# Last layer's output projection as seven block products instead of eight, with the weight sums on GpSimd and VectorE

## The reference, cut to what matters

```python
for l in range(DEPTH):                       # DEPTH = 2
    xn = rms_norm(h, norm_g[l])
    proj = xn @ w_in[l]
    ...                                      # three head groups: ya, yb, yc; gates ga, gb, gc
    mixed = concatenate([ya * silu(ga), yb * silu(gb), yc * silu(gc)])
    h = h + mixed @ w_out[l]                 # (528 x 2048) @ (2048 x 2048)
return h[:, REAL_START:]                     # the 512 real positions only
```

## Time and profile before

| | us |
|---|---|
| median of 3 runs (lowest, highest) | 1549.18 (1548.6, 1549.85) |
| span of the profiled execution | 1547.2 |
| TensorE busy | 1537.9 (99%) |
| VectorE busy | 949.6 (61%) |
| ScalarE (ACT) busy | 646.1 (42%) |
| GpSimd (POOL) busy | 197.0 (13%) |
| DMA traffic over the span | 97 GB/s |

### The profile page before, as it was taken

One profiled execution on the slowest core, in us unless ns is written; L12 is line 12 of the kernel. 1 busy time (PEld: TensorE's weight loads), 2 busy tenths in 40 slices (PEclk: granted clock), 3 DMA queues, 4 the chain that ended last, 5 costly groups with the idle time before them and its releaser, 6 DMA issues.

```text
span 1547.2 us, 26370 instructions
## 1 busy us (share of the span) xinstructions
PE 1537.9 (99%) x10458; PEld 1423.5 (92%) x10458; DVE 949.6 (61%) x1829; ACT 646.1 (42%) x1291; POOL 197.0 (13%) x348
## 2 busy tenths in 40 slices
PE   8999999999999999999999999999999999999999
PEld 7999999999999999999998889888999888888888
DVE  5787788677778444343336676876777774442322
ACT  5776566612333332322236665666132343221211
POOL 0112654400000000000000016544000000000000
PEclk9999999999999999999999999999999999999999
DMA  7222111223221322443342231121223123234442
GB/s 279 102 83 82 56 55 58 73 74 99 82 84 55 105 86 97 139 151 124 130 146 86 82 109 56 55 78 60 86 80 110 55 82 109 82 133 141 142 146 69
DMA packets 39739, 151.79 MB, mean 98 GB/s; under 512 B 5424, under 2 KB 14400, under 8 KB 24896
## 3 DMA queue, kind: packets, MB, share of 16 engines
...
## 4 chain that ended last, share of the span: by engine, by line
PE 96%; DVE 1%; issue 1%; POOL 1%; ACT 1%; DMA 0%; ACTq 0%; DVEq 0%; POOLq 0%
PE ps_gemm L1144 82%; PE ps_mix L1031 3%; PE ps_mix L950 2%; PE ps_mix L996 2%; PE ps_gemm L911 2%; PE ps_mix L964 2%; PE ps_gemm L1105 1%; PE ps_gemm L898 1%; PE ps_mix L898 1%; PE ps_mix L992 1%; PE ps_mix L1074 1%; PE ps_mix L1089 1%; PE ps_mix L1091 0%; DMA w_stage<-in_w_in 0%; PE ps_mix L977 0%
## 5 line engine op out<-in xcount | busy, mean ns | idle before, releaser
L1144 PE MATMUL ps_gemm<-x_hi,w_hi 128*128 128x264 f32 (+3 forms) x2176 | 542.2, 314 | 0.2 <-issue 0.2
L1144 PE MATMUL ps_gemm<-x_hi,w_lo 128*128 128x264 f32 (+3 forms) x2176 | 528.3, 308 | 0.0
L1144 PE MATMUL ps_gemm<-x_lo,w_hi 128*128 128x264 f32 (+3 forms) x2176 | 527.6, 307 | 0.0
L1144 PEld LDWEIGHTS ps_gemm<-x_hi,w_hi 128*128 128x128 f32 x2176 | 353.8, 189 | 19.8 <-issue 0.6
L1144 PEld LDWEIGHTS ps_gemm<-x_hi,w_lo 128*128 128x128 f32 x2176 | 352.1, 188 | 19.3
L1144 PEld LDWEIGHTS ps_gemm<-x_lo,w_hi 128*128 128x128 f32 x2176 | 351.5, 188 | 16.8
L647 ACT ACTIVATE w_hi<-w_stage 128x512 fp32r<-128x512 f32 x464 | 267.1, 618 | 172.0 <-DVE z L1309 122.8
L1216 DVE TENSOR_TENSOR w_lo<-w_stage,w_hi 128x512 fp32r<-128x512 f32 x392 | 259.5, 690 | 82.2 <-ACT w_hi L647 76.3
L1144 PE MATMUL ps_gemm<-mixed_hi,w_lo 128*128 128x264 f32 (+1 forms) x752 | 199.0, 320 | 0.0
L1144 PE MATMUL ps_gemm<-mixed_lo,w_hi 128*128 128x264 f32 (+1 forms) x752 | 198.7, 320 | 0.0
L1144 PE MATMUL ps_gemm<-mixed_hi,w_hi 128*128 128x264 f32 (+1 forms) x752 | 197.6, 318 | 0.0
...
## 6 DMA issues: line engine op xcount, KB each, us to landing
w_stage<-in_w_in SPq DMA_DIRECT2D x82, 1024.0 KB, 4.9
w_stage<-in_w_out SPq DMA_DIRECT2D x32, 1024.0 KB, 5.4
...
a_rden<-rden SPq DMA_DIRECT2D x32, 128.0 KB, 5.0
...
```

The source lines that it names most:

```text
L1144: ins = pe.matmul(g[:, bank, 0:size], ws, xs[:, k, c:c + size], start=tick == 0 and i == 0, stop=tick == TICKS - 1 and i == 2)
```

## The change

In the last layer (`FAST`) the output projection is no longer a run of chunks. The weight is cut into 8 pairs p of row blocks (output channels 256p to 256p + 255), each pair into four quarters of 128 output channels by 1024 contraction rows (A11, A12, A21, A22; 512 KB each). The data is cut the same way, contraction halves (`K_FIRST`, `K_SECOND`) by time halves of 256 positions (B11, B12, B21, B22). Each pair is then made from seven block products of 8 x 3 matmuls of 256 columns, in place of eight (a Winograd variant of Strassen's form):

- sums of the data, made once: T1 = B12 - B11 (VectorE, in `gate_product`, in the place of B12), T2 = B22 - T1 and T4 = B21 - T2 (GpSimd, `t_raws`), T3 = T2 - B11 (GpSimd, `t3_raw`);
- sums of the weights, for each pair: S1 = A21 + A22, S3 = A11 - A21, S4 = A12 - S2 (GpSimd, `sum_1`, `sum_3`, `sum_4`), S2 = S1 - A11 (VectorE, `sum_2`);
- the products, in this order: A11 B11, S1 T1, S2 T2, S4 B22, S3 T3, A12 B21, A22 T4. Bank x gathers A11 B11, S2 T2, S3 T3 and A22 T4 one on the other, bank z S1 T1 and S4 B22; VectorE takes the bank out after each of them (`product_out`, 7 for a pair) and adds it to the residual or to what stands in z.

Each of the seven weights goes through a high part on ACT (`out_high`) and a low part on VectorE (`out_low`), now in one piece of 1024 columns each; so do T2, T3, T4 (`t_high`, `t_low`). The raw quarters and sums lie in a ring of 12 places, the high parts in one of 4. The eager order of all this around the last gate chunk (N = 99) and in pair 0 is written out by hand. The diff, cut to its core:

```diff
--- before.py
+++ after.py
-NTOT = DEPTH * NC
...
+FAST = DEPTH - 1
+NTOT = NC * FAST + N_IN
+HALF_K = KC // 2
+K_FIRST, K_SECOND = GATES[:HALF_K], GATES[HALF_K:]
+PAIRS = KC // 2
+HALF_T = SEQ // 2
+PRODUCTS = ("a11", "s1", "s2", "s4", "s3", "a12", "a22")
+NPROD = len(PRODUCTS)
+RING, HI_RING = 12, 4
+RING_AT = {"a11": 0, "s1": 1, "a21": 2, "s3": 2, "a22": 3, "s2": 4, "a12": 5, "s4": 6}
...
+        def bank_of(p, which):
+            b = (3 * p + "xzy".index(which)) % 4
+            return G[:, b // 2, b % 2, 0:HALF_T]
...
+            sp.wait_ge(s_gemm, NTOT - 2)
+            load_quarter(0, "a21")
+            load_quarter(0, "a22")
+            sp.wait_ge(s_gemm, NTOT - 1)
+            load_quarter(0, "a11")
+            sp.wait_ge(s_xfree, 1)
+            load_quarter(0, "a12")
+            load_quarter(1, "a11")
...
+            sp.wait_ge(s_hy, 4 * DEPTH)
+            load_res(0, 0)
+            load_res(0, 1)
+            sp.wait_ge(s_gemm, NTOT)
+            load_quarter(1, "a21")
+            sp.wait_ge(s_t3r, 2)
+            sp.wait_ge(s_tlo["t2"], 2)
+            load_quarter(1, "a22")
+            for p in range(PAIRS):
+                if p + 1 < PAIRS:
+                    sp.wait_ge(s_made, made(p, "a11"))
+                    load_quarter(p + 1, "a12")
+                sp.wait_ge(s_out, made(p, "s2"))
+                if p + 1 < PAIRS:
+                    load_res(p + 1, 0)
+                if p + 2 < PAIRS:
+                    load_quarter(p + 2, "a21")
+                sp.wait_ge(s_out, made(p, "s4"))
+                store_quarter(p, 0, 1)
+                if p + 2 < PAIRS:
+                    sp.wait_ge(s_made, made(p, "s3"))
+                    load_quarter(p + 2, "a11")
+                sp.wait_ge(s_out, made(p, "s3"))
+                store_quarter(p, 1, 1)
+                if p + 2 < PAIRS:
+                    sp.wait_ge(s_made, made(p, "a12"))
+                    load_quarter(p + 2, "a22")
+                sp.wait_ge(s_out, made(p, "a12"))
+                store_quarter(p, 0, 0)
+                sp.wait_ge(s_out, made(p, "a22"))
+                store_quarter(p, 1, 0)
+                if p + 1 < PAIRS:
+                    load_res(p + 1, 1)
+            for i in range(2):
+                for j in range(2):
+                    sp.wait_ge(s_q[i][j], 16 * PAIRS)
...
+            def t_raws(N):
+                zi, j = N % 2, K_SECOND.index(gate_of(N % NC))
+                m = K_FIRST[j]
+                if j == 0:
+                    pool.wait_ge(s_hy, 4 * DEPTH)
+                    pool.wait_ge(s_rdm, 8 * DEPTH)
+                    pool.wait_ge(s_rdo, 16 * DEPTH)
+                pool.wait_ge(s_prod, KC * FAST + HALF_K + j + 1)
+                pool.wait_ge(s_mlo, KC * FAST + j + 1)
+                z1, z2 = zq(zi, 0), zq(zi, 1)
+                link(pool.tensor_tensor(t2r[:, j], z2, mh[:, m, t_half(1)].bitcast(F32), ALU.subtract))
+                link(pool.tensor_tensor(t2r[:, j], t2r[:, j], ml[:, m, t_half(1)].bitcast(F32), ALU.subtract))
+                pool.tensor_tensor(t4r[j // 4][:, j % 4], z1, t2r[:, j], ALU.subtract).then_inc(s_traw, 1)
+            def t3_raw(half):
+                js, ms = slice(4 * half, 4 * half + 4), slice(K_FIRST[4 * half], K_FIRST[4 * half] + 4)
+                if half == 0:
+                    pool.wait_ge(s_gemm, NTOT)
+                link(pool.tensor_tensor(t3r[:, js], t2r[:, js], mh[:, ms, t_half(0)].bitcast(F32), ALU.subtract))
+                link(pool.tensor_tensor(t3r[:, js], t3r[:, js], ml[:, ms, t_half(0)].bitcast(F32), ALU.subtract))
+                pool.sem_inc(s_t3r, 1)
+            def sum_1(p):
+                pool.wait_ge(s_ld["a21"][p % 2], 16 * (p // 2 + 1))
+                pool.wait_ge(s_ld["a22"][p % 2], 16 * (p // 2 + 1))
+                if p >= 2:
+                    pool.wait_ge(s_made, made(p - 2, "a22"))
+                else:
+                    pool.wait_ge(s_gemm, NTOT - 1 + p)
+                pool.tensor_tensor(raw_of(p, "s1")[:], raw_of(p, "a21")[:], raw_of(p, "a22")[:], ALU.add)\
+                    .then_inc(s_sum["s1"], 1)
...
+            def sum_3(p):
+                pool.wait_ge(s_ld["a11"][p % 2], 16 * (p // 2 + 1))
+                pool.wait_ge(s_sum["s1"], p + 1)
+                pool.tensor_tensor(raw_of(p, "s3")[:], raw_of(p, "a11")[:], raw_of(p, "a21")[:], ALU.subtract)\
+                    .then_inc(s_sum["s3"], 1)
+            def sum_4(p):
+                pool.wait_ge(s_ld["a12"][p % 2], 16 * (p // 2 + 1))
+                pool.wait_ge(s_sum["s2"], p + 1)
+                if p:
+                    pool.wait_ge(s_made, made(p - 1, "s1"))
+                else:
+                    pool.wait_ge(s_xfree, 1)
+                pool.tensor_tensor(raw_of(p, "s4")[:], raw_of(p, "a12")[:], raw_of(p, "s2")[:], ALU.subtract)\
+                    .then_inc(s_sum["s4"], 1)
...
+                    if layer == FAST and tick == T_RAW_TICK and n and gate_of(n - 1) in K_SECOND:
+                        t_raws(N - 1)
+                if N == NTOT - 1:
+                    sum_1(0)
+                    sum_3(0)
+                    sum_4(0)
+            t3_raw(0)
+            t_raws(NTOT - 1)
+            t3_raw(1)
+            for p in range(1, PAIRS):
+                sum_1(p)
+                sum_3(p)
+                sum_4(p)
...
+            def out_high(p, name):
+                no = made(p, name) - 1
+                if name in s_sum:
+                    act.wait_ge(s_sum[name], p + 1)
+                else:
+                    act.wait_ge(s_ld[name][p % 2], 16 * (p // 2 + 1))
+                if no >= HI_RING:
+                    act.wait_ge(s_made, no - HI_RING + 1)
+                else:
+                    act.wait_ge(s_gemm, NTOT - 1 + no // 2)
+                act.activation(high[no % HI_RING], raw_of(p, name)[:], ACT.Copy).then_inc(s_ohi, 1)
...
+            out_high(0, "s1")
+            out_high(0, "a11")
+            act.wait_ge(s_xfree, 2)
+            act.wait_ge(s_traw, HALF_K - 1)
+            t_high("t2", 0, HALF_K - 1)
+            out_high(0, "s2")
+            N = NTOT - 1
+            zz = zs(N % 2)[:, N_META:T]
+            act.wait_ge(s_z, N + 1)
+            act.activation(ta_[:, N_META:T], zz, ACT.Tanh, scale=0.5).then_inc(s_th, 1)
+            out_high(0, "s4")
+            act.wait_ge(s_prod, KC * DEPTH)
+            act.activation(mh[:, GATES[-1], N_META:T], zz, ACT.Copy).then_inc(s_mhi, 1)
+            act.wait_ge(s_traw, HALF_K)
+            t_high("t2", HALF_K - 1, HALF_K)
+            act.wait_ge(s_t3r, 1)
+            t_high("t3", 0, 4)
+            out_high(0, "s3")
+            t_high("t4", 0, 4)
+            t_high("t4", 4, 8)
+            act.wait_ge(s_t3r, 2)
+            t_high("t3", 4, 8)
+            out_high(0, "a12")
+            out_high(0, "a22")
+            for p in range(1, PAIRS):
+                for name in PRODUCTS:
+                    out_high(p, name)
...
+            def product(p, name):
+                which, cols, moving = {"a11": ("x", 0, "first"), "s1": ("z", 1, "first"), "s2": ("x", 0, "t2"),
+                                       "s4": ("z", 1, "second"), "s3": ("x", 0, "t3"), "a12": ("y", 0, "second"),
+                                       "a22": ("x", 0, "t4")}[name]
+                no = made(p, name) - 1
+                pe.wait_ge(s_olo, no + 1)
+                if name == "a11" and p >= 2:
+                    pe.wait_ge(s_out, made(p - 2, "a12"))
+                if name == "s1" and p:
+                    pe.wait_ge(s_out, made(p - 1, "a22"))
+                if name in ("s2", "s4", "s3"):
+                    pe.wait_ge(s_out, no - 1)
+                if name == "a12":
+                    if p:
+                        pe.wait_ge(s_out, made(p - 1, "s4"))
+                    else:
+                        pe.wait_ge(s_z, NTOT)
+                if name == "a22":
+                    pe.wait_ge(s_out, made(p, "s3"))
+                start = name in ("a11", "s1", "a12")
+                o = bank_of(p, which)
+                hi, lo = high[no % HI_RING], low[ring_at(p, name)]
+                for j in range(HALF_K):
+                    if moving in th_:
+                        if p == 0 and j in (0, 4, 7):
+                            pe.wait_ge(s_tlo[moving], {0: 1, 4: 1 if moving == "t2" else 2, 7: 2}[j])
+                        xs, ys = th_[moving][:, j], tl_[moving][:, j]
+                    else:
+                        m = (K_FIRST if moving == "first" else K_SECOND)[j]
+                        if p == 0 and name == "s4" and j == HALF_K - 1:
+                            pe.wait_ge(s_mlo, KC * DEPTH)
+                        xs, ys = mh[:, m, t_half(cols)], ml[:, m, t_half(cols)]
+                    for i, (ws, vs_) in enumerate(((hi[:, j], xs), (hi[:, j], ys), (low[ring_at(p, name)][:, j], xs))):
+                        ins = pe.matmul(o, ws, vs_, start=start and j == 0 and i == 0,
```

(92 more changed lines are left out.)

111 lines of the change are left out of this document (69 added, 42 removed).

## The result

The kernel after takes 1555.79 us (median of 4 runs, 1554.67 to 1556.41), the kernel before on the same chip 1548.89 (4 runs, 1547.36 to 1549.85): a ratio of 1.0043, 95% interval 1.0031 to 1.0055. The forecast was 1554.5. The profiled execution has a span of 1553.9 us (1547.2 before).

The account below looks back on a forecast made before the run. TensorE, busy 99% of the span, was taken as the bound. The terms -19.1 + 22.2 + 1.5 + 0.8 = +5.4 us took the median from 1549.18 to about 1554.5, range 1538 to 1563.

Parts of the forecast that it names:

- the turns: VectorE operations with two SBUF inputs and GpSimd sums exclude each other, each for a whole operation; said to decide the forecast.
- the walk: Diff's order timed operation by operation through the projection's start: TensorE begins 8.2 us after 1366.1, pair 1 at 1408.2.
- the signs named in advance: Pair 0 stretched to 34 us, out_low and t_low up to 3.5 us beside sums of up to 3.6.
- TensorE's own work: Projection matmuls: 178.2 us removed, 159.1 added, net -19.1 us if every product finds its operands ready.
- The beginning: Projection's start, pair 0: sums and low parts made in turns while TensorE needs only 19.9 us; 22.2 us lost.
- Pair 1 and the clock: Pair 1's start: 1.5 us where sum_1(2) cuts in before S1's low part, 0.8 for TensorE's lowered clock.
- The edits that cost nothing: Gate slots and tail: T1's subtracts (8 x 0.42 us) and t_raws fall in idle time; tail as before.
- The smaller tile: Projection matmuls of 256 columns: half the columns cost 51% of the time, taking back 3.5 of 22.3 us.
- The first: Rival: engines don't exclude each other at these places; VectorE alone paces the beginning, -12.5 us, 1536.7; chance 0.15.
- The second: Rival: GpSimd's float32 sums run at the fast rate, 1.9 us for 1024 columns; 1547, halfway 1550.5; chance 0.20.
- The third: Rival: turns bind in every pair, 20.5 to 21.2 us instead of 19.9; 1558 to 1563; chance 0.15.
- The fourth: Rival: the whole 19.1 us saving of the projection arrives; 1530; chance 0.02.

Follow-up runs that it names:

- Experiment 1: Kernel after, but out_low, t_low and sum_2 read their second input from PSUM (other data) instead of SBUF: 1540.91 us, 0.9944 of before.
- 4: Kernel after with T3's four GpSimd subtracts cut to 4 columns, T3's parts made from T4's tile: 1549.39 us, one run.
- 2: Kernel after with S1, S3, S4 and T3 computed on VectorE, its order changed too: 1546.24 us, 0.9980 of before.
- experiment 3: Kernel after without the eight T1 subtracts in gate_product, B12 standing in for T1: 1555.22 us, one run.
- 5: Kernel with S1, S3, S4 and T3 on VectorE, pair 0 now done as eight plain block products: 1539.46 us, 0.9935 of before.
- experiment 6: Kernel with the plain first pair, pair 1's A11 low part now made first in its own buffer, S3 later: 1538.46 us, 0.9928 of before.

## Why the prediction was right

**The step that decides, the turns.** It was taken from pieces of 512 columns for pieces of 1024 and 1792. Every time of the walk came 0.9 to 1.4 us after its forecast, a nearly constant shift from the first entry on: S1 done at 1364.3 (forecast 1363.1), S4 at 1370.2 (1369.0), the first half of T3 at 1374.3 (1373.1), TensorE's start at 1375.4 (1374.3), pair 1 at 1409.3 (1408.2). From S1 to pair 1 the walk had 45.1 us and the trace has 45.0. Experiment 1 shows the mechanism, 4 that the length of that exclusive work sets the end, and in 2, with the sums on one engine, the low parts are back at 1.23 on average. The turns don't fill the whole stretch: GpSimd sat idle 3.95 us, until 1394.61, for the load of pair 1's weights and 5.45 us before S4 of pair 1, while VectorE worked on alone. The walk has both (`sum_1(1)` ends at 1396.0 there, at 1397.0 in the trace). The widest rows were longer than the signs named in advance, 4.03 for the 3.5 of `t_low` and 4.12 for the 3.6 of a sum, where each waited for a full operation of the other engine. The rule of the Trainium skill (SBUF — State Buffer, Who interferes with whom: an operation with at most one SBUF input doesn't contend, one with two contends with GpSimd's reads, and the port pair is an exclusive lock) held at the widths seen here, 512 to 1792 columns: for 1024 columns 1.22 us in experiment 1 against a mean of 1.75 in the kernel after.

**The terms of the sum.** In the projection the forecast was -19.1 + 22.2 + 1.5 + 0.8 = +5.4; the trace has 183.73 - 178.16 = +5.6.
- TensorE's own work: -19.1 forecast, -18.3 measured (eight steady pairs of 19.98). The steady pitch is 0.1189, not the 0.1184 of `last_block`, 0.08 us a pair, 0.7 in all; a product is 2.84 to 2.88.
- The beginning: 22.2 forecast. Measured 8.3 before the first product and 33.86 - 19.98 = 13.9 of stretch in pair 0, together 22.2.
- Pair 1 and the clock: 1.5 + 0.8 forecast; pair 1 lost 21.69 - 19.98 = 1.7. The clock did fall to its lower level, before the first product and near the end of the pair, and A11's product took 5.28 us and A22's 4.42. But both lie in pair 0, where VectorE was later still; the 0.8 put ahead for pair 1's start did not come here (it did in experiments 2 and 5, where A11's product in pair 1 took 4.24 and 5.28). The two errors, +0.8 in TensorE's own work and -0.6 here, nearly cancel: that the sum is off by only 0.2 is partly luck.
- "The edits that cost nothing": this step failed. T1's subtracts were costed at 0 because VectorE sits idle before each take-out of a gate chunk. That is true around the last gates, but the earlier ones lie beside the attention, where TensorE waits for VectorE; experiment 3 shows 1.4 to 1.5 us of the 3.4. In the profiled execution 0.5 of it is hidden by a start that was 0.5 earlier than in before's. So the change of the span is 6.7: 1.5 - 0.5 ahead of the projection, 5.6 in it, and 0.1 in the tail; and the median came 1.3 above the forecast.
- Two smaller slips change nothing in the sum. The smaller tile takes back 22.3 - 19.1 = 3.2 us, not 3.5. And GpSimd's 2.15 ns a column stands in no row of the kernel before; the kernel after bears it out, with 0.74 us for 256 columns and 2.40 for 1024.

**The rivals.** The first (no exclusion, 1536.7) is nearly what experiment 1 built: 1540.9. Its first product came 4.3 us after the gate, not 3.6, and the clock fell there too (0.81 from 1366 to 1375, A11's product 4.50 us), which the rival's sum left out. The second, GpSimd at its fast rate, is out: 2.40 by itself, for 2.38 forecast; the estimate of 2.25 from the GPSIMD Engine Reference of the Trainium skill would have been 6% low for these operands. The third, turns that bind in every pair, is out: pair 2 to pair 7 take 19.98 with the sums on either engine. The turns are still there, in every pair, but there is more room for them than the forecast said. Pair 4 in the kernel after:
```profile
1471.00:1491.00 20.00, 20.00 (x170) 20.00 (x170) 15.92 (x15) 7.43 (x7) 9.69 (x3) 1.00 0.50 160
```
Three of its seven PSUM reads lie beside a sum, as the forecast had it; three of its low parts last 1.73, 2.25 and 2.86 us; and VectorE still sits idle for 4.1 of the 20 us, where the forecast had it nearly full. The fourth, the whole 19.1, needs a cover for the start-up; experiment 6, with an ordinary first pair, gets 12.9 of it.
